# Six more weight slots for the experts, and the mLSTM chores spread over 26 steps of the windowed attention

## The reference

```python
h = rmsnorm(x, norm1_g)
qa, ka, va, qm, km, vm, om, gm, mg = split_cols(h @ w_in, IN_SPLITS)
ya = windowed_gqa(qa, ka, va, ...)          # 8 heads, window 128, T5 bias, sink
ym = mlstm_branch(qm, km, vm, om, gm, ...)  # conv of 5 taps, silu, two scans, 4 heads
gates = sigmoid(mg + merge_b)
u = gates[:, :1024] * (ya @ w_branch_attn) + gates[:, 1024:] * (ym @ w_branch_mlstm)
x = x + u @ w_out
# hier_moe: best of 4 groups, best 2 of its 8 experts for each token
x = x + sum over both experts of weight * (silu(t @ w_gate[e]) * (t @ w_up[e])) @ w_down[e]
```

## Time and profile before

| | |
|---|---|
| median of 3 runs | 2285.16 us (2284.2 to 2285.91) |
| the profiled execution | 2284.88 us, span 2283.0 us, mean granted clock 0.955 |
| TensorE busy | 2037.0 us (89%) |
| VectorE, ScalarE, GpSimd busy | 672.9, 590.4, 678.4 us |
| moved by DMA | 362.43 MB, of which 192 requests of 1 MB are expert weights |
| windowed attention, steps 0 to 31 | 1305 to 1552 us |
| last product of the output projection | 1718 us |
| experts, first product to last | 1774.0 to 2256 us |

### The profile page before, as it was taken

How to read it: one execution, slowest core, us unless ns; L and a number is a source line. 1 busy time by engine, 2 the same in 40 slices (tenths; PEclk the granted TensorE clock), 3 DMA queues, 4 the chain that set the end, 5 groups by cost and what they waited for, 6 DMA issues and landing times.

```text
span 2283.0 us, 29374 instructions
## 1 busy us (share of the span) xinstructions
PE 2037.0 (89%) x10746; PEld 1446.5 (63%) x10747; DVE 672.9 (29%) x1145; ACT 590.4 (26%) x987; POOL 678.4 (30%) x383
## 2 busy tenths in 40 slices
PE   8987899999999999999999989997893887778884
PEld 7864688888888878888887756775782322222221
DVE  2348631110052243111007685124546000000002
ACT  2126333332212222333221325444420000000000
POOL 4421134444514434444451522222230000000000
PEclk9998999999999999999999989999896899999997
DMA  7311023332313324333231311210116899999996
GB/s 213 108 56 39 19 93 101 94 99 93 130 54 95 105 77 121 101 92 101 92 129 45 117 56 56 65 56 19 55 62 242 342 426 427 427 426 426 425 423 242
DMA packets 155405, 362.43 MB, mean 159 GB/s; under 512 B 16671, under 2 KB 88991, under 8 KB 130752
## 3 DMA queue, kind: packets, MB, share of 16 engines
q1 hardware_dynamic: 142880, 341.35, 40.5%
q10 hardware_dynamic: 7664, 11.64, 1.9%
q0 software_dynamic: 4784, 8.40, 1.0%
HBM read 355.58 MB, written 14.68 MB: 162 GB/s over the span
## 4 chain that ended last, share of the span: by engine, by line
PE 68%; DMA 16%; DVE 12%; issue 2%; ACT 1%; POOL 1%; SPq 0%; POOLq 0%; DVEq 0%; ACTq 0%
PE ps L1755 19%; PE ps L1757 18%; PE ps L1756 18%; DMA wpair<-l_expert 14%; PE ps L2239 5%; PE ps L2170 1%; DVE hres L1131 1%; DVE qkm L1406 1%; PE ps L2105 1%; DVE nmax L1209 1%; PE ps L2127 1%; POOL wlo L981 1%; DMA xg<-x2d,nowi 1%; DVE attn L1219 1%; PE ps L2151 1%
## 5 line engine op out<-in xcount | busy, mean ns | idle before, releaser
L981 POOL TENSOR_TENSOR wlo<-wraw,whi 128x1024 fp32r<-128x1024 f32 (+2 forms) x244 | 574.0, 2357 | 959.5 <-ACT whi L615 958.9
L1755 PE MATMUL ps<-xhi,whi 128*128 128x512 f32 (+2 forms) x1196 | 463.8, 388 | 3.2 <-ACT som L839 2.5
L1757 PE MATMUL ps<-xhi,wlo 128*128 128x512 f32 (+2 forms) x1196 | 460.5, 385 | 0.0
L1756 PE MATMUL ps<-xlo,whi 128*128 128x512 f32 (+2 forms) x1196 | 460.2, 385 | 0.0
L615 ACT CAST whi<-wraw 128x1024 fp32r<-128x1024 f32 (+2 forms) x244 | 245.9, 1014 | 608.0 <-PE ps L1757 581.4
L2239 PE MATMUL ps<-wpair,mx 128*32 128x512 f32 (+1 forms) x2048 | 249.9, 637 | 73.4 <-DMA wpair<-l_expert 72.1
L1755 PEld LDWEIGHTS ps<-xhi,whi 128*128 128x128 f32 x1196 | 226.2, 189 | 50.4 <-issue 7.5
L1757 PEld LDWEIGHTS ps<-xhi,wlo 128*128 128x128 f32 x1196 | 225.9, 189 | 44.1
L1756 PEld LDWEIGHTS ps<-xlo,whi 128*128 128x128 f32 x1196 | 226.2, 189 | 43.0
L2239 PEld LDWEIGHTS ps<-wpair,mx 128*32 128x32 f32 x2048 | 75.1, 116 | 247.2 <-issue 246.7
L1064 POOL COPY nowi<-idx 128x1 uint32 (+1 forms) x33 | 6.2, 187 | 479.5 <-DVE ybuf L1727 430.0
(11 more groups left out here) (403 smaller groups left out, 2370.7 us busy)
## 6 DMA issues: line engine op xcount, KB each, us to landing
wpair<-l_expert SPq DMA_DIRECT2D x192, 1024.0 KB, 25.4
wraw<-ffn_w_gate SPq DMA_DIRECT2D x88, 256.0 KB, 2.8
wraw<-ffn_w_up SPq DMA_DIRECT2D x88, 256.0 KB, 3.0
wraw<-ffn_w_down SPq DMA_DIRECT2D x44, 512.0 KB, 3.5
wraw<-w_in SPq DMA_DIRECT2D x36, 512.0 KB, 3.5
wraw<-attn_w_qkv SPq DMA_DIRECT2D x24, 512.0 KB, 9.1
wraw<-conv_w_in SPq DMA_DIRECT2D x96, 128.0 KB, 2.2
wraw<-attn_w_o SPq DMA_DIRECT2D x8, 512.0 KB, 3.5
```

What stands on the lines that cost most here:

```text
L981: pool.tensor_tensor(l, wraw[:, s, :, 0:cols], h.bitcast(F32), ALU.subtract).then_inc(w_lo, 1)
L1755: pe.matmul(dst, ahi, bhi, start=start, stop=False)
L1756: pe.matmul(dst, ahi, blo, start=False, stop=False)
L1757: return pe.matmul(dst, alo, bhi, start=False, stop=stop)
```

## The change

It has three parts. Six extra slots (`wextra`, in three pairs `epair`) lie where `xhi`, `xlo` and `scr` are free by then, and in one place of the arena. The small routing tiles that stood there move to other places. Pass 1 takes slots 0 to 5 from the extras and 6 to 11 from `wexp[0..5]`, pass 2 takes `wexp[6..11]` and the extras, pass 3 and later take `wexp` in order. Its requests go out earlier, in the order below, and expert 17 stands first in pair 1 whatever the counts are. TensorE has passes 0 to 2 written out. In the windowed attention the gate operations are done two per step (steps 0 to 5), the taps two per step (steps 6 to 25), and the Silus four each in steps 18 and 27.

```diff
@@ placement
         wpair = [place(f"wpair{n}", [P, 2, 4 * BANKF], F32, ae) for n in range(SLOTS // 2 - 1)]
-        rest = [ae[0]]
+        far = (ae[0] - at_scr) // 4
         ae[0] += 4 * BANKF * 4
+        epair = [place("epair0", [P, 2 * 4 * BANKF], F32, [base + 3 * RING * 2 * BANKF * 4]),
+                 place("epair1", [P, 2 * 4 * BANKF], F32, [base + 3 * RING * 2 * BANKF * 4 + 16384]),
+                 place("epair2", [P, far + 4 * BANKF], F32, [at_scr])]
+        estep = (4 * BANKF, 4 * BANKF, far)
+        wextra = [epair[n // 2][:, n % 2 * estep[n // 2]:n % 2 * estep[n // 2] + 4 * BANKF] for n in range(6)]
...
-        el = place("el", [P, TILES, EXPERTS], F32, rest)
+        el = place("el", [P, TILES, EXPERTS], F32, ae)
...
@@ SyncE
-                sp.wait_ge(w_used, pair[0])
...
-                load_experts(EXPERTS // 2, 0)
+                def load(dst, s, ea, eb, done):
+                    src = wx[bass.ds(eb if s % 2 else ea, 1), s // 2, :, :].rearrange("e p n -> p (e n)")
+                    sp.dma_start(dst, src).then_inc(done, 16)
+
+                early = (EXPERTS // 2 + 1, 1)
+                sp.wait_ge(u_lo, 2)
+                for s in range(4, 10):
+                    load(wexp[s][:, :], s, EXPERTS // 2, 0, m_loaded[s])
+                load(wextra[5], 5, *early, m_extra[5])
+                sp.wait_ge(w_used, pair[0])
+                for s in (0, 1, 2, 3, 10, 11):
+                    load(wexp[s][:, :], s, EXPERTS // 2, 0, m_loaded[s])
+                sp.wait_ge(logits_full, 1)
+                for s in range(4):
+                    load(wextra[s], s, *early, m_extra[s])
+                for n in range(2):
+                    sp.wait_ge(x2_stored[n], 32)
+                load(wextra[4], 4, *early, m_extra[4])
                 sp.wait_ge(routed, 1)
...
-                with sp.Fori(0, more) as i:
+                for s in range(6, SLOTS):
+                    sp.wait_ge(m_used, s - 6 + 1)
+                    load(wexp[s - 6][:, :], s, *early, m_loaded[s - 6])
+                ea, eb = expert(4), expert(5)
+                for s in range(SLOTS):
+                    if s < 6:
+                        sp.wait_ge(m_used, s + 6 + 1)
+                        load(wexp[s + 6][:, :], s, ea, eb, m_loaded[s + 6])
+                    else:
+                        sp.wait_ge(m_used, SLOTS + s - 6 + 1)
+                        load(wextra[s - 6], s, ea, eb, m_extra[s - 6])
+                ea, eb = expert(6), expert(7)
+                for s in range(SLOTS):
+                    sp.wait_ge(m_used, SLOTS + s + 6 + 1)
+                    load(wexp[s][:, :], s, ea, eb, m_loaded[s])
+                with sp.Fori(3, more) as i:
                     load_experts(expert(i * 2 + 2), expert(i * 2 + 3), i)
@@ ScalarE, windowed attention
-                if 10 <= k < 14:
-                    for n in range(2 * (k - 10), 2 * (k - 10) + 2):
+                if k in (18, 27):
+                    for n in range(MH) if k == 18 else range(MH, 2 * MH):
@@ VectorE, windowed attention (gate_scan and conv now do a third and one tap of their work)
-                if k < 2:
-                    gate_scan(k)
-                elif k < 10:
-                    conv(k - 2)
+                if k < 6:
+                    gate_scan(k // 3, k % 3)
+                elif k < 6 + MH * TAPS:
+                    for n in range(2 * (k - 6), 2 * (k - 6) + 2):
+                        conv(n // TAPS, n % TAPS)
@@ VectorE, routing
-            run(dve.memset(first_heavy[:, 0:1], 1.0))
+            run(dve.memset(first_heavy[:, 0:2], 1.0))
@@ TensorE, experts (hidden, outputs and expert_pass take the slots from slot_of and wait by wait_loaded)
+            def slot_of(n, s):
+
+                if isinstance(n, int) and n == 1:
+                    return (None, s) if s < 6 else (s - 6, None)
+                if isinstance(n, int) and n == 2:
+                    return (s + 6, None) if s < 6 else (None, s - 6)
+                return s, None
...
+            for n in range(3):
+                turn(n)
+            with pe.Fori(2, more) as i:
+                turn(i + 1)
```

More of the change, by code:

```diff
@@ L288, in build @@
         sel = place("sel", [P, TOP * TILES, P], F32, [base + 4096])
+        befl = place("befl", [P, MORE, EXPERTS], F32, [base + 8192])
         blk1 = place("blk1", [P, TOP * TILES, 2, PAIRS], F32, ae)
@@ L298, in build @@
         second = place("second", [P, PAIRS], I32, ae)
-        befl = place("befl", [P, MORE, EXPERTS], F32, ae)
         bef = place("bef", [P, MORE + 4], F32, ae)
@@ L435, in build @@
         m_used = sem("m_used")
+        m_extra = [sem(f"m_extra{n}") for n in range(6)]
         idx_now = sem("idx_now")
@@ L1398, in _, with conv @@
             ck, cv, bf, qmk = Count(cols_kept), Count(conv_done), Count(bank_free), Count(qm_kept)
-            def conv(n):
+            def conv(n, k):
                 m, c = divmod(n, MH)
                 y = qkm[:, n, :]
[L1403 to L1406, removed]
+                tap = vecs[:, V_CONV + n * TAPS + k:V_CONV + n * TAPS + k + 1]
+                if k == 0:
+                    run(dve.tensor_scalar(y, cpad[m][:, c, 0:SEQ], tap, None, ALU.mult))
+                else:
+                    run(dve.scalar_tensor_tensor(y, cpad[m][:, c, k:k + SEQ], tap, y, ALU.mult, ALU.add), cv if k == TAPS - 1 else step)
@@ L2251, in hidden @@
                         for half in range(2):
-                            pe.wait_ge(m_loaded[s + half], n * 16 + 16)
+                            wait_loaded(n, s + half)
                         for c in range(4):
-                            expert_pass(bank, mx, 4 * quad + c, DC, s, c * BANKF, first, inc=c == 3)
+                            expert_pass(n, bank, mx, 4 * quad + c, DC, s, c * BANKF, first, inc=c == 3)
             def turn_tokens(n):
@@ L2274, in outputs, with turn @@
                     for half in range(2):
-                        pe.wait_ge(m_loaded[s + half], n * 16 + 16)
+                        wait_loaded(n, s + half)
                     for c in range(2):
                         for wide in range(2):
-                            expert_pass(2 + wide, mhT, 2 * duo + c, D_EXP // P, s, (2 * c + wide) * BANKF, first, inc=c == 1 and wide == 1)
-            turn_tokens(0)
-            first = wider_of(0)
-            hidden(0, first)
-            turn_tokens(1)
-            turn_hidden(0)
-            outputs(0, first)
-            with pe.Fori(0, more) as i:
-                first = wider_of(i + 1)
-                hidden(i + 1, first)
-                turn_tokens(i + 2)
-                turn_hidden(i + 1)
-                outputs(i + 1, first)
+                            expert_pass(n, 2 + wide, mhT, 2 * duo + c, D_EXP // P, s, (2 * c + wide) * BANKF, first, inc=c == 1 and wide == 1)
+            def turn(n):
+                first = wider_of(n)
+                hidden(n, first)
+                turn_tokens(n + 1)
+                turn_hidden(n)
+                outputs(n, first)
+            turn_tokens(0)
+            for n in range(3):
+                turn(n)
+            with pe.Fori(2, more) as i:
+                turn(i + 1)
 V_QG, V_KG, V_GATE = 0, 1, 2
```

45 lines of the change are left out of this document (31 added, 14 removed).

## The result

| | before | after |
|---|---|---|
| median | 2285.53 us (2284.2 to 2289.49, 4 runs) | 2250.22 us (2249.42 to 2252.74, 4 runs) |
| profiled execution | 2284.88 us, span 2283.0 | 2249.42 us, span 2247.6 |

The ratio is 0.9845, 95% interval [0.9827, 0.9862]: 35 us less, against 2248.4 us predicted. Timed once more in a later set of runs, the changed kernel gave 0.9863 [0.984, 0.9886].

What follows compares the result with a forecast made beforehand. TensorE's waits for VectorE in the windowed attention and for expert weights were taken to bound the kernel. 2284.88 - 22.0 (chores) - 14.8 (slots) = 2248.1, with the median 0.28 above: 2248.4 us; range 2242 to 2264.

Steps and rivals of the forecast that it cites:

- Chores: Windowed attention: gate operations and taps in portions, with later Silus, save 22.0 us of 26.8 us excess.
- 1, 3, 6 and 14: Windowed attention steps: 1, 3 and 6 lose their excess (16.0 us); 14 loses 4.1 us by moving Silus.
- step 5: Windowed attention: keeps 1.1 to 2.8 us of excess, since step 4's gate portion meets a GpSimd split.
- step 9: Windowed attention: keeps the turn of eight columns and a wait for their copy, 1.8 to 3.9 us.
- Steps 21 and 23: Windowed attention: no loss priced; maximum to scaling of 3.2 us, 5.2 if blocked, fits every two-portion step (7.3 or 7.8).
- The block: VectorE beside GpSimd splits: maximum and taps end 2.4 us after the maximum starts, ahead of the split at 2.8, unblocked.
- a sign that it had named as wrong: Windowed attention: TensorE waiting for the scaled probabilities in steps 11, 13, 20 and 22 would show the forecast wrong.
- Rival (a): Six one-portion attention steps each blocked, 0.7 us late plus perhaps 2.6 from slow clock: up to 20 us, 2264; chance 0.13.
- The slots: Expert stage: six extra slots leave 174 requests instead of 180 behind 1780, 6 x 2.46 = 14.8 us less.
- the stream doesn't dry up: Expert weight queue: about 3 us in hand at its thinnest; the opposing rival, slots giving nothing, 2263, had chance 0.10.
- TensorE's first wait for weights: Expert stage: said to come in pass 5, not 3, as a sign that the forecast holds.
- The added instructions: TensorE's written-out expert passes, about 800 instructions: put at nothing, at most a microsecond for each of four fetches.

Runs made afterwards that it cites:

- e1: The changed kernel without its chores in portions and late Silus, keeping extra slots, earlier requests and written-out passes: 2267.3 us, ratio 0.994.
- e7: e1 with the six requests for extra slots moved behind the first wait for a slot of pass 0: 2285.23 us, ratio 1.0002.
- e10: The kernel before, twelve slots, with requests 4 to 9 sent at the second half of ulo, near 1680 instead of 1718: 2284.42 us, ratio 1.0.
- e2: The changed kernel without its expert part, only chores in portions and late Silus: 2263.7 us, ratio 0.9927.
- e5: The changed kernel run again unchanged, for comparison: 2250.77 us, ratio 0.9863.
- e9: e7 without its wait, so all six extra requests go out when routing ends: 2272.05 us, ratio 0.995.
- e3: The kernel before with only the Silus moved, four each in steps 18 and 27: 2280.17 us, ratio 0.9987.
- e8: e1 with three of the six extra requests (extras 3 to 5) moved late, extras 0 to 2 left ahead of routing: 2276.57 us, ratio 0.9968.
- e11: The kernel before with its whole chores moved from between maximum and scaling to behind the scaling: 2284.87 us, ratio 1.0001.
- e4: The changed kernel with each step's portion of chores behind the scaling instead of between maximum and scaling: 2247.1 us, ratio 0.986.
- e6: The changed kernel with chores only in steps with two portions of products, Silus in steps 19 and 28: 2248.08 us, ratio 0.9849.

## Why the prediction was right

**Chores (22.0 us predicted).** The pair of profiled executions shows 240.7 - 216.7 = 24.0 us, but both ends vary with the clock, and the one before, from which the prediction was read, is the longest of six. Six executions with the old attention (before, e1, e7 to e10) have 238.5 us in the mean, three with the new (after, e2, e5) 217.8: 20.7 us, inside the predicted 20.1 to 23.9. By steps, in the pair: 1, 3, 6 and 14 gave 6.0, 5.5, 5.4 and 4.1, as priced, but for step 1, whose bare length is 6.5 and not the 7.3 that I took; step 5 kept 1.2 (predicted 1.1 to 2.8; 2.9 in e2), step 9 kept 1.5 (predicted 1.8 to 3.9; 3.1 in e5). Steps 21 and 23 lost 0.5 each, which the prediction put at nothing. One reading of the prediction needs a correction. Step 5 of the kernel before "kept the full clock: it lost 2.8 us where step 3 lost 5.4", but that was no saving: there and in e9, the two executions in which it did so, TensorE waited 2.7 us in step 6 as well, and the two steps took 22.8 us; in e1, e3, e7, e8 and e10 step 5 ran at a mean clock of 0.73 (12.7 to 12.9 us), step 6 had no wait, and the two took 20.2.

**The block.** That the maximum and a portion of taps end just ahead of the split, and stay unblocked, is what the trace shows (no fused tap above 0.754 us). The step that failed is the next one: the scaling that stands behind the portion was priced as if nothing could meet it, and it is what the split blocks. So a sign that it had named as wrong did show: TensorE waits for the scaled probabilities of steps 20 and 22, though not for those of 11 and 13. Rival (a) had the block in each of six one-portion steps; it fell in three, and costs 1.2, 0.5 and 0.5 us in the profile of the change, not 0.7 + 2.6 each. Only the 1.1 us of steps 21 and 23 stood outside the sum; had the clock fallen behind these two waits as it did behind that of step 5 in e2 (2.9 us in all), it would have been more, so in this the forecast had luck. By the rule of the Trainium skill (SBUF — State Buffer, "SBUF: two separate sides") the later of two such operations waits for the whole instruction of the earlier. The trace agrees with it here too: a blocked addition of 128x1 (two SBUF inputs) is done when the split is, 2.23 us for 0.16.

**The slots (14.8 us predicted).** Five executions with twelve slots have 504.5 us in the mean (before, e2, e3, e10, e11), five with 18 MB in ahead of the first freed slot have 490.3 (after, e1, e4, e5, e6): 14.2 us, or 2.37 for one of the six requests, for 2.46. The mechanism, fewer megabytes behind the first freed slot, is shown from both sides by e7, e8 and e10. That the stream doesn't dry up is in the profile: its 30th request lands at 1843, the engines are 1.01 busy from 1830 to 1850, and 1.01 from 1880 to 2200. TensorE's first wait for weights came in the last half of pass 4, where I had said pass 5. The added instructions cost little: e7, which has them and nothing early, has an expert stage of 505.7 us, 0.8 to 1.9 more than the five with twelve slots; no run separates the instructions from the order of requests.

**What the sum didn't hold.** In the pair the mLSTM stage is 2.6 us longer after (73.9 to 76.5). It isn't the change: with either attention ahead of it this stage lies between 72.9 and 76.9 us, and it is 76.9 in e1, with the old one. What differs is the clock. Busy time of this stage in the kernel before and in the changed one:

```profile
1554.50:1628.40 73.90, 56.33 (x232) 39.84 (x232) 39.11 (x83) 36.10 (x112) 16.74 (x12) 0.84 0.09 29
...
1530.80:1607.30 76.50, 58.95 (x232) 41.25 (x233) 39.28 (x83) 36.10 (x112) 16.77 (x12) 0.80 0.08 28
```

TensorE is idle for 17.6 us in both, and busy for 2.6 more at the lower clock; in e4 the clock is 0.86 and the stage 73.0. So the pair reads 24.0 - 2.6 + 14.3 = 35.7 (35.4 us of span), and the means 20.7 + 14.2 = 34.9. The predicted 22.0 + 14.8 = 36.8 was 1.9 us too much, and the median is 1.8 above the forecast. One claim was tested in part: with expert 17 in front there are 16 passes as before (16 Silus of the experts), but no run here has the old order with the new slots.

## What to carry to other kernels

When an engine feeds another through a chain (maximum, scaling), cut the work that sits in between until the chain fits the shortest step, and put it in steps with room; moving it behind the chain only shifts the wait to the next thing queued on that engine. When a stage ends with a stream of weights, count the bytes that land before the first slot comes free: only those shorten it, by the queue's own pace, and early requests without slots or slots filled late give nothing. Compare such kernels by the lengths of their stages over several executions: with the same instructions the old attention varied by 3.9 us and the mLSTM stage by 4.0, as much as one long step cost.

## What the runs showed of the hardware

- The price of a short wait isn't fixed. The same 1.17 us of TensorE in step 5 left the clock at 1.00 in two executions (8.5 us) and brought it to 0.83 in a third (10.1 us); 1.05 us in step 9 gave 9.3 or 10.9 us. With the old attention, and its long waits, six executions lie between 236.8 and 240.7 us.
- Being small doesn't spare a VectorE operation beside a GpSimd split of 2.4 to 2.8 us: an addition of 128x1 went from 0.16 us to 2.23, a scaling of 128x256 from 0.35 to 2.38, a scan of 4x512 on four partitions from 1.22 to 3.27. Others pass: the maximum with an input in a bank of TensorE (0.48 us) and an operation of 128x1 on its result (0.15 us) ran inside a split at their usual length. Which property frees the second one, no run here separates.
- A gather of GpSimd that starts with six 1 MB transfers just ahead of it in the queues landed 9.0 us after its issue (e9), against 4.5 in empty ones (the changed kernel); in the full stream of the changed kernel TensorE waited 2.40, 0.90 and 1.66 us for the gathers at the turns of passes 2 to 4.
